# Expert queries of a hybrid decoder step: weights stationary, turned queries straight from the projection

## The chip, the cores and the metric

The kernel runs on one core of a Trainium2 chip. The metric is the device time of one launch in microseconds, the median of several runs; less is better. Matrix products run on TensorE (PE, its weight loads PEld), element-wise work on VectorE (DVE) and ScalarE (ACT), the gathers of expert rows are issued by GpSimd (POOL), and most plain loads by SyncE (SP). All transfers share the core's 16 DMA engines.

## The reference

One layer of a decoder: a token mixer (short convolution and dilated window attention), then a product-key expert layer, for 1024 prompt tokens and 64 sample tokens of width 1024. What the change touches is the expert layer:

```python
def block(xb):                                   # 128 tokens
    q = (xb @ w_query).reshape(PEER_BLOCK, PEER_HEADS, 2, half)      # 8 heads, 2 halves of 128
    s1 = jnp.einsum('thd,kd->thk', q[:, :, 0], sub_keys[0])
    s2 = jnp.einsum('thd,kd->thk', q[:, :, 1], sub_keys[1])
    v1, i1 = lax.top_k(s1, PEER_TOPK)
    v2, i2 = lax.top_k(s2, PEER_TOPK)
    ...                                          # best 16 of the 256 sums -> eidx, gate
    act = jnp.einsum('td,thkd->thk', xb, expert_u[eidx])
    coef = gate * jax.nn.gelu(act)
    return jnp.einsum('thk,thkd->td', coef, expert_v[eidx])
```

Every token reads 8 x 16 rows of `expert_u` and as many of `expert_v`, 4 KB each.

## The kernel before, in words

After a front part (conditioning, first norm, attention inputs), the function `peer` runs everything else as two programs that share the engines.

The **foreground** is 72 jobs, one for each of 9 token tiles (tile 2 holds the 64 sample tokens twice, and its 8 jobs have 8 rows for each partition instead of 16) and 8 heads. Job s ranks scores into expert indices (DVE, `experts`), gathers a u row and a v row for every rank (POOL, lines 1501 and 1511, rings of 8 slots each, u and v alternating in one queue), takes dot products with the u rows (DVE, line 2443), and adds the v rows of job s-1 with their coefficients. About half of the v rows are added by DVE (line 2459), the others by PE as products with a diagonal matrix that ACT makes (line 2107 makes it, line 1787 is the product, 4 records for a row). A v slot comes free when its row is added; a POOL gather that waits for one holds back the gathers behind it.

The **background** makes what the jobs need, in three segments of three tiles: norm, input projections and attention (segments 1 and 2; segment 0's are made in the front part), convolution, `mix`, output projection `out` (line 1729), second norm, `turn` (line 1714, which turns a normed tile into `hT`), and the queries. Its pieces are numbered by `chain_order`, which sets the order on PE, ACT and DVE alike and gives each piece one of six PSUM banks in turn. `Pace` lets each engine go as far into that order as `limit(s, f)` allows at fraction f of job s: `chain_cost` gives each piece a cost, and marks tie job numbers to pieces (everything up to score 6 comes ahead of job 0, the first score of segment g by job 24g - 3, all by job 51). An engine that reaches a piece waits in place, with the rest of its program behind it.

The second norm of a tile is a chain over engines: `add_x` (DVE) after the tile's three `out` chains, `root` (ACT; it also waits until the tile before is stored), `shift_tile` (DVE, last instruction line 2354), then `turn` (PE) and `keep_turned` (ACT). SP stores each tile (`store_tile`) after its shift.

Queries: an item is one head of one tile, and `it` counts them, head by head and within a head tile by tile. In step i, `queries` projects item i with the tile as the stationary operand (line 1756, 8 products of 256 columns, 16 records), ACT copies the result to `qn` (line 2036), PE turns the item before (line 1765, two transposes), ACT copies it to `qT` (line 2044), PE scores the item before that against the sub-keys (line 1773), and ACT copies the scores to one of two `sc_out` buffers (line 2052) and stores them. The third tile's `turn` stands behind the second projection. `load_scores` (line 2063) reads them back for a job. The query weights come in eight blocks of 1 MB, one for each head, by SP (line 1401) into a ring of three slots.

## Time and profile before

| | |
|---|---|
| median of 3 runs | 4194.48 us (4192.9 to 4195.76) |
| profiled execution | 4189.91 us, span 4187.2 us |
| mean granted TensorE clock | 0.882 of full speed |
| busy share of the span | PE 78%, DVE 69%, POOL 59%, PEld 42%, ACT 15% |
| moved by DMA | 1405 MB, mean 336 GB/s |

The profile describes one execution. Its page gives busy time by engine, the span in slices, the chain of work that ended last and groups of instructions; the trace behind it can be asked for stretches (windows), for single instructions in order of time (timeline), and for who waited for whom. A PE row's length holds the pipeline's tail, so the distance between starts tells what a chain takes. The DMA share is the mean busy share of 16 engines; in stretches where transfers never stop it reads up to 1.05.

### The profile page before, as it was taken

Reading aid. Unit: us, or ns where it says so; the run is one execution under the profiler, and the core shown is the slowest. Engines: PE = TensorE matmul, PEld = TensorE weight load, DVE = VectorE, ACT = ScalarE, POOL = GpSimd, SP = SyncE. Lnnn points to the kernel's source line nnn. Section 1 sums busy time; section 2 is a strip of 40 time slices with the busy share of each in tenths; the row PEclk is TensorE's granted clock in tenths of the full one; section 3 lists DMA queues with packets and bytes.
Section 4 is the critical chain, followed back from the end, with each engine's and each line's share of the span. In section 5 each row is a group of like instructions: output and inputs, shape, how many; then the busy total and the mean of one; then the engine's idle time right before and its main releaser. Section 6 shows DMA issues by size and latency. Waiting matters only on the chain. (4 is left out here: it accounts for less than half of the span.)

```text
span 4187.2 us, 33973 instructions
## 1 busy us (share of the span) xinstructions
PE 3280.6 (78%) x9782; PEld 1758.2 (42%) x9798; DVE 2895.2 (69%) x6507; ACT 635.6 (15%) x1759; POOL 2488.9 (59%) x2277
## 2 busy tenths in 40 slices
PE   6978898788888987788888888887777666566666
PEld 1445575654444544455444445444444222222222
DVE  2212111678786777988878987787778788778875
ACT  0020001221012212123110133111111111101010
POOL 0001000477764677567787666876777777777775
PEclk9968898899997899889998898998888888988888
DMA  7316344799997999999999989999999999999998
GB/s 257 124 34 174 98 121 150 277 403 403 393 387 255 331 387 396 352 391 376 401 402 390 385 320 335 390 391 387 387 393 391 373 409 409 408 409 397 405 409 323
DMA packets 578893, 1405.09 MB, mean 336 GB/s; under 512 B 44731, under 2 KB 276347, under 8 KB 578683
## 3 DMA queue, kind: packets, MB, share of 16 engines
q0 software_dynamic: 320080, 1165.57, 71.7%
q1 hardware_dynamic: 223070, 196.45, 15.0%
q10 hardware_dynamic: 35560, 40.91, 2.8%
q8 instruction: 81, 1.33, 0.1%
q14 instruction: 102, 0.84, 0.1%
HBM read 1369.31 MB, written 33.44 MB: 335 GB/s over the span
## 5 line engine op out<-in xcount | busy, mean ns | idle before, releaser
L1787 PE MATMUL peer_psA<-peer_vring,peer_diag 128*128 128x512 f32 x2464 | 1394.8, 706 | 626.4 <-DMA peer_vring<-in_expert_v,peer_idx 474.3
L1501 POOL DMA_INDIRECT peer_uring<-in_expert_u,peer_idx x1088 | 1224.4, 1125 | 713.6 <-DVE peer_idx L2416 360.7
L1511 POOL DMA_INDIRECT peer_vring<-in_expert_v,peer_idx x1088 | 1222.4, 1124 | 548.2 <-issue 301.0
L2443 DVE CUSTOM_DVE_ANT_0 peer_uring<-peer_uring,peer_h 128x1024 f32<-128x1024 f32 x768 | 934.6, 1217 | 218.7 <-DMA peer_uring<-in_expert_u,peer_idx 217.0
L1787 PEld LDWEIGHTS peer_psA<-peer_vring,peer_diag 128*128 128x128 f32 x2464 | 509.6, 221 | 1353.2 <-issue 1165.3
L2459 DVE SCALAR_TENSOR_TENSOR peer_acc<-peer_vring,peer_coef,peer_acc 128x1024 f32<-128x1024 f32 x463 | 593.9, 1283 | 86.2 <-DMA peer_vring<-in_expert_v,peer_idx 80.7
L2443 DVE CUSTOM_DVE_ANT_0 peer_uring<-peer_uring,peer_psB 128x1024 f32<-128x1024 f32 x320 | 388.8, 1215 | 142.8 <-DMA peer_uring<-in_expert_u,peer_idx 142.5
L1682 PE MATMUL peer_psB<-keep_hT,peer_w 128*128 128x384 f32 (+1 forms) x864 | 279.2, 483 | 12.2 <-DMA peer_w<-in_w_in 12.2
L1756 PE MATMUL peer_psB<-peer_w,keep_hT 128*128 128x256 f32 x1152 | 273.4, 393 | 18.4 <-DMA peer_w<-in_w_query 17.3
L1700 PE MATMUL peer_psB<-keep_hT,peer_w 128*128 128x384 f32 (+1 forms) x768 | 250.8, 482 | 20.8 <-DMA peer_w<-in_w_attn_o 20.8
L1756 PEld LDWEIGHTS peer_psB<-peer_w,keep_hT 128*128 128x128 f32 x1152 | 228.5, 200 | 76.5 <-issue 28.2
L2149 ACT ACTIVATE peer_g<-peer_g 128x16 f32<-128x16 f32 (+1 forms) x72 | 15.5, 215 | 1459.7 <-DVE peer_g L2473 1459.7
L1682 PEld LDWEIGHTS peer_psB<-keep_hT,peer_w 128*128 128x128 f32 x864 | 170.4, 198 | 125.8 <-issue 23.9
L1700 PEld LDWEIGHTS peer_psB<-keep_hT,peer_w 128*128 128x128 f32 x768 | 150.4, 197 | 121.4 <-DMA peer_w<-in_w_attn_o 25.0
L2107 ACT ACTIVATE peer_diag<-keep_ident,peer_coef 128x128 f32<-128x128 f32 x616 | 187.8, 388 | 59.8 <-DVE peer_coef L2483 59.8
L1579 PE MATMUL peer_psB<-peer_w,keep_hT 128*128 128x384 f32 x576 | 196.4, 496 | 0.0
L1579 PEld LDWEIGHTS peer_psB<-peer_w,keep_hT 128*128 128x128 f32 x576 | 113.0, 197 | 88.1 <-issue 23.4
L1729 PE MATMUL peer_psB<-peer_w,peer_mT 128*128 128x384 f32 (+3 forms) x432 | 130.6, 461 | 3.0 <-DVE peer_mT L2325 3.0
L1637 PE MATMUL peer_psB<-peer_w,peer_arena 128*128 128x64 f32 x576 | 89.2, 314 | 37.7 <-ACT peer_arena L1967 37.7
L1614 PE MATMUL peer_psB<-peer_w,peer_mT 64*128 64x512 f32 (+3 forms) x224 | 104.9, 552 | 3.4 <-issue 1.8
L1637 PEld LDWEIGHTS peer_psB<-peer_w,peer_arena 128*128 128x128 f32 x576 | 86.3, 232 | 49.1 <-issue 44.6
L1729 PEld LDWEIGHTS peer_psB<-peer_w,peer_mT 128*128 128x128 f32 (+1 forms) x432 | 81.7, 190 | 56.1 <-issue 17.2
(245 smaller groups left out, 2943.8 us busy)
## 6 DMA issues: line engine op xcount, KB each, us to landing
peer_w<-in_w_in SPq DMA_DIRECT2D x102, 512.0 KB, 21.8
peer_w<-in_w_query SPq DMA_DIRECT2D x24, 1024.0 KB, 15.7
peer_w<-in_w_in SPq DMA_DIRECT2D x12, 1536.0 KB, 18.4
peer_uring<-in_expert_u,peer_idx POOLq DMA_INDIRECT x1088, 10.7
peer_vring<-in_expert_v,peer_idx POOLq DMA_INDIRECT x1088, 10.6
front_ring<-in_w_ada POOLq DMA_DIRECT2D x7, 2048.0 KB, 8.3
front_ring<-in_w_ada SPq DMA_DIRECT2D x5, 2048.0 KB, 7.8
peer_w<-in_w_conv_o SPq DMA_DIRECT2D x24, 384.0 KB, 23.1
```

What stands on the lines that cost most here:

```text
L1501: pool.indirect_dma_start(out=uring[:, r % U, :], out_offset=None, in_=io["expert_u"], in_offset=bass.IndirectOffsetOnAxis(ap=idx[:, s % 4 ...
L1511: pool.indirect_dma_start(out=vring[:, r % V, :], out_offset=None, in_=io["expert_v"], in_offset=bass.IndirectOffsetOnAxis(ap=idx[:, s % 4 ...
L1579: last = pe.matmul(dst[:, 0:WQKV], hT[:, k, i * P:(i + 1) * P], wv[:, k, :], start=(k == 0), stop=(k == DC - 1))
L1637: last = pe.matmul(bank(key_o)[:, 0:HD], pT[:, t_slot[g, it, b] % 2, (at % 4) * P:(at % 4 + 1) * P], vv[:, kb, col:col + HD], start=(at == ...
L1682: last = pe.matmul(dst[:, 0:m], wv[:, k, part, :], hT[:, k, 0:m], start=(k == 0), stop=(k == DC - 1))
L1700: last = pe.matmul(dst[:, 0:m], wv[:, KC_AT[q] + k, :], src[:, k, 0:m], start=(k == 0), stop=(k == KC[q] - 1))
L1729: last = pe.matmul(dst[0:R, 0:e - a], mT[:, k, i * P:i * P + R], wv[:, k, :], start=(k == 0), stop=(k == DC - 1))
L1756: last = pe.matmul(dst[:, 0:KD], hT[:, k, j * P:(j + 1) * P], wv[:, k, :], start=(k == 0), stop=(k == DC - 1))
L1787: last = pe.matmul(psA[:, c * 512:(c + 1) * 512], diag[:, a % DG, :], vring[:, r % V, c * 512:(c + 1) * 512], start=first, stop=False, ski ...
L2107: act.activation(diag[:, a % DG, :], ident[:], ACT.Copy, scale=coef[:, s % 4, k:k + 1]).then_inc(diag_set, 1)
L2443: dve.tensor_tensor_reduce(uring[:, r % U, :], uring[:, r % U, :], rows, 1.0, 0.0, ALU.mult, ALU.add, act_[:, k:k + 1]).then_inc(u_used, 1)
L2459: dve.scalar_tensor_tensor(out=acc[:], in0=vring[:, r % V, :], scalar=c, in1=acc[:], op0=ALU.mult, op1=ALU.add).then_inc(v_added, 1)
```

## The change

A head's query weights become the stationary operand: one chain makes one half (128 query columns) of one head for all three tiles, 384 columns at once, and the result comes out turned. So 24 projections of 256 columns and 24 pairs of transposes in a segment become 16 chains `("query", g, h, c)` of 384 columns; `qn` and the transposes go, and ACT copies 16 results of 384 columns to `qT`, where it copied 48 of 256. `qT` now holds four heads and lies in `mT`, the input of the output projection. Scores are still taken by item: the first two of head h-1 stand between the two chains of head h, the third behind them. As a chain reads all three tiles, the third tile's `turn` moves ahead of all queries. `sc_out` has four buffers, and `chain_cost` has 5.1 for a query where it had 3.4 for a projection and 0.5 for a turn.

```diff
+SO = 4
...
-        for i in range(n + 2):
-            if i == 2:
-                order += [("turn", g, SEG - 1, c) for c in range(2)]
-            order += [(name, first + i - lag) for lag, name in enumerate(("project", "turn_q", "score"))
-                      if 0 <= i - lag < n]
+        order += [("turn", g, SEG - 1, c) for c in range(2)]
+        for h in range(HEADS + 1):
+            if h < HEADS:
+                order += [("query", g, h, 0)]
+            order += [("score", (g * HEADS + h - 1) * SEG + i) for i in range(2 if h else 0)]
+            if h < HEADS:
+                order += [("query", g, h, 1)]
+            if h:
+                order += [("score", (g * HEADS + h - 1) * SEG + 2)]
...
-    return {"project": 3.4, "qkv": 5.1, "s": 1.2, "o": 1.5, "t": 0.6}.get(name, 0.5)
+    return {"query": 5.1, "qkv": 5.1, "s": 1.2, "o": 1.5, "t": 0.6}.get(name, 0.5)
...
-    return "project", (g * HEADS + j) * SEG + SEG - 1
+    return "query", g, j, 1
...
-        qn, qT, sc_out = n.sb("qn", [P, 2, K2]), n.sb("qT", [P, 2, K2]), n.sb("sc_out", [P, 2, K2])
+        sc_out = n.sb("sc_out", [P, SO, K2])
+        QS = 4
+        qT = flat[:, 0:QS * 2 * M].rearrange("p (s c m) -> p s c m", s=QS, c=2)
...
             def queries(g):
...
-                        for k in range(DC):
-                            last = pe.matmul(dst[:, 0:KD], hT[:, k, j * P:(j + 1) * P], wv[:, k, :],
-                                             start=(k == 0), stop=(k == DC - 1))
...
-                        for c in range(2):
-                            last = pe.transpose(dst[:, c * P:(c + 1) * P], qn[:, it % 2, c * P:(c + 1) * P], ident[:])
...
+                    for i in range(SEG):
+                        wait_emptied(pe, ("turn", g, i, 1))
+                    dst = opened(key)
+                    for k in range(DC):
+                        last = pe.matmul(dst[:, 0:M], wv[:, k, c * P:(c + 1) * P], hT[:, k, :],
+                                         start=(k == 0), stop=(k == DC - 1))
...
+                yield from turn(g, SEG - 1)
+                for h in range(HEADS + 1):
+                    if h < HEADS:
+                        yield from query(h, 0)
+                    if h:
+                        yield from score(h - 1, 0)
+                        yield from score(h - 1, 1)
+                    if h < HEADS:
+                        yield from query(h, 1)
+                    if h:
+                        yield from score(h - 1, 2)
...
             def norm_root(g, i):
-                yield number["score", (g - 1) * SEG * HEADS + 5 + 5 * i]
+                yield number["score", (g - 1) * SEG * HEADS + 5 + 6 * i]
...
             def keep_queries(g):
...
+                    if h >= QS:
+                        wait_filled(act, ("score", (g * HEADS + h - QS) * SEG + SEG - 1))
+                    act.activation(qT[:, h % QS, c, :], bank(key)[:, 0:M], ACT.Copy).then_inc(out_of(key), 1)
...
+                    if it >= SO:
+                        act.wait_ge(sc_stored[it % SO], 16 * (it // SO))
+                    act.activation(sc_out[:, it % SO, :], bank(key)[:, 0:K2], ACT.Copy).then_inc(out_of(key), 1)
...
             def shift_tile(g, i):
...
-                yield number["out", g, i + 1, 0] if i + 1 < SEG else number["project", g * SEG * HEADS]
+                yield number["out", g, i + 1, 0] if i + 1 < SEG else number["turn", g, SEG - 1, 0]
```

Where this moves instructions on PE, at three places. In these rows line numbers are each kernel's own: before, 1714 is `turn`, 1729 `out`, 1739 the convolution's tail, 1756 the projection, 1765 the transposes, 1773 the scores, 1787 the sum of v rows; after, they are 1721, 1736, 1746, 1759, none, 1770 and 1796. `peer_qT` and `peer_mT` are the turned queries.

Segment 0, ahead of the first job, from the second tile's `turn` on. Before:

```order
L1714 MATMUL peer_psB<-keep_ident,peer_arena 128x128 x8
L1756 MATMUL peer_psB<-peer_w,keep_hT 128x256 x16
L1765 MATMUL peer_psB<-keep_ident,peer_qn 128x128 x2
L1714 MATMUL peer_psB<-keep_ident,peer_arena 128x64 x8
L1756 MATMUL peer_psB<-peer_w,keep_hT 128x256 x8
L1765 MATMUL peer_psB<-keep_ident,peer_qn 128x128 x2
L1773 MATMUL peer_psB<-peer_skT,peer_qT 128x128 x2
L1756 MATMUL peer_psB<-peer_w,keep_hT 128x256 x8
L1765 MATMUL peer_psB<-keep_ident,peer_qn 128x128 x2
```

After:

```order
L1721 MATMUL peer_psB<-keep_ident,peer_arena 128x128 x8
L1721 MATMUL peer_psB<-keep_ident,peer_arena 128x64 x8
L1759 MATMUL peer_psB<-keep_hT,peer_w 128x384 x24
L1770 MATMUL peer_psB<-peer_skT,peer_mT 128x128 x4
L1759 MATMUL peer_psB<-keep_hT,peer_w 128x384 x8
L1770 MATMUL peer_psB<-peer_skT,peer_mT 128x128 x2
L1759 MATMUL peer_psB<-keep_hT,peer_w 128x384 x8
```

The third tile's turn (128x64 x8) goes from behind two projections to ahead of all queries; and score 6, the last piece ahead of job 0, stands behind seven chains of 384 columns, where it stood behind nine of 256.

Segment 1, from the second tile's `turn` on. Before:

```order
L1729 MATMUL peer_psB<-peer_w,peer_mT 128x256 x8
L1714 MATMUL peer_psB<-keep_ident,peer_arena 128x128 x8
L1756 MATMUL peer_psB<-peer_w,keep_hT 128x256 x16
L1765 MATMUL peer_psB<-keep_ident,peer_qn 128x128 x2
L1714 MATMUL peer_psB<-keep_ident,peer_arena 128x128 x8
L1787 MATMUL peer_psA<-peer_vring,peer_diag 128x512 x6
```

After:

```order
L1736 MATMUL peer_psB<-peer_w,peer_mT 128x256 x8
L1721 MATMUL peer_psB<-keep_ident,peer_arena 128x128 x4
L1796 MATMUL peer_psA<-peer_vring,peer_diag 128x512 x2
L1721 MATMUL peer_psB<-keep_ident,peer_arena 128x128 x12
L1796 MATMUL peer_psA<-peer_vring,peer_diag 128x512 x6
L1759 MATMUL peer_psB<-keep_hT,peer_w 128x384 x16
L1796 MATMUL peer_psA<-peer_vring,peer_diag 128x512 x6
```

The third tile's turn follows the second's at once (x12 is half of one and all of the other), and three v rows (x6) stand between it and the first queries.

Segment 2, from the second tile's `turn` on. Before:

```order
L1714 MATMUL peer_psB<-keep_ident,peer_arena 128x128 x8
L1739 MATMUL peer_psB<-keep_ident,peer_tail 18x128 x4
L1787 MATMUL peer_psA<-peer_vring,peer_diag 128x512 x2
L1739 MATMUL peer_psB<-keep_ident,peer_tail 18x128 x2
L1787 MATMUL peer_psA<-peer_vring,peer_diag 128x512 x2
L1756 MATMUL peer_psB<-peer_w,keep_hT 128x256 x8
L1787 MATMUL peer_psA<-peer_vring,peer_diag 128x512 x2
L1756 MATMUL peer_psB<-peer_w,keep_hT 128x256 x8
L1765 MATMUL peer_psB<-keep_ident,peer_qn 128x128 x2
L1714 MATMUL peer_psB<-keep_ident,peer_arena 128x128 x8
L1787 MATMUL peer_psA<-peer_vring,peer_diag 128x512 x6
```

After:

```order
L1721 MATMUL peer_psB<-keep_ident,peer_arena 128x128 x8
L1746 MATMUL peer_psB<-keep_ident,peer_tail 18x128 x6
L1721 MATMUL peer_psB<-keep_ident,peer_arena 128x128 x8
L1796 MATMUL peer_psA<-peer_vring,peer_diag 128x512 x4
L1759 MATMUL peer_psB<-keep_hT,peer_w 128x384 x8
L1796 MATMUL peer_psA<-peer_vring,peer_diag 128x512 x4
L1759 MATMUL peer_psB<-keep_hT,peer_w 128x384 x8
L1796 MATMUL peer_psA<-peer_vring,peer_diag 128x512 x6
```

Two v rows (x2 each) and two projections stood between the second and the third turn; now only the tail's transposes do.

## Rows read from the trace of the kernel before

**Rows 1.** The page, part 2: transfer rate in forty equal slices (about 104.7 us each).

```profile
GB/s 257 124 34 174 98 121 150 277 403 403 393 387 255 331 387 396 352 391 376 401 402 390 385 320 335 390 391 387 387 393 391 373 409 409 408 409 397 405 409 323
```

**Rows 2.** Windows (us): busy us (instructions) of PE, PEld, DVE, ACT, POOL, PEclk, DMA share, GB/s.

```profile
1240.00:1420.00 180.00, 157.89 (x545) 85.63 (x549) 130.81 (x314) 47.65 (x143) 91.08 (x84) 0.79 0.78 277
1420.00:1700.00 280.00, 238.21 (x674) 128.04 (x674) 223.37 (x499) 48.56 (x109) 208.29 (x173) 0.95 1.05 392
1774.00:1990.00 216.00, 174.84 (x683) 122.61 (x684) 181.46 (x436) 59.18 (x155) 148.33 (x123) 0.89 1.00 383
2400.00:2600.00 200.00, 173.94 (x699) 100.77 (x709) 161.26 (x375) 61.17 (x181) 122.83 (x112) 0.87 0.88 318
2900.00:2920.00 20.00, 7.80 (x20) 3.84 (x20) 12.23 (x25) 3.91 (x7) 6.66 (x7) 0.72 0.81 311
2954.00:3262.00 308.00, 234.97 (x769) 142.42 (x770) 241.14 (x531) 56.37 (x172) 244.66 (x208) 0.87 1.01 391
```

**Rows 3.** Timeline before the first gather: start us, us, engine, line, operation [idle before <-releaser].

```profile
720.49 1.22 DVE L2354 TENSOR_TENSOR peer_arena<-peer_arena 64x1024 f32<-64x1024 f32 x1
...
721.82 10.08 PE L1756 MATMUL peer_psB<-peer_w,keep_hT 128*128 128x256 f32 x32 [9.62 <-DMA peer_w<-in_w_query]
...
732.05 0.71 PE L1714 MATMUL peer_psB<-keep_ident,peer_arena 64*128 64x64 f32 x8
...
732.54 1.21 ACT L2019 ACTIVATE keep_hT<-peer_psB 128x256 f32<-128x256 f32 x4
...
738.05 3.62 PE L1756 MATMUL peer_psB<-peer_w,keep_hT 128*128 128x256 f32 x16
...
741.72 0.61 PE L1773 MATMUL peer_psB<-peer_skT,peer_qT 128*128 128x128 f32 x4
...
742.17 3.62 PE L1756 MATMUL peer_psB<-peer_w,keep_hT 128*128 128x256 f32 x16
...
762.30 29.32 SPq L1401 DMA_DIRECT2D peer_w<-in_w_query  x2
...
762.32 0.61 PE L1773 MATMUL peer_psB<-peer_skT,peer_qT 128*128 128x128 f32 x4
...
764.24 1.04 ACTq L2063 DMA_DIRECT2D peer_sc<-key_scores  x2
...
770.01 0.49 DVE L2367 MAX8 peer_v<-peer_sc 128x8 f32<-128x128 f32 x2 [5.92 <-DMA peer_sc<-key_scores]
```

**Rows 4.** Timeline, PE: an output projection chain of 384 columns in segment 1.

```profile
1740.76 5.33 PE L1729 MATMUL peer_psB<-peer_w,peer_mT 128*128 128x384 f32 x16
```

**Rows 5.** Window of 5 us at the first query projection (columns as in the windows above).

```profile
720.00:725.00 5.00, 3.18 (x8) 2.56 (x9) 1.68 (x2) 0.00 (x0) 0.00 (x0) 0.50 1.09 349
```

**Rows 6.** Groups by line and form from 700 us: xcount | busy, mean ns | idle before, releaser.

```profile
L2052 ACT ACTIVATE peer_sc_out<-peer_psB 128x256 f32<-128x256 f32 x72 | 27.4, 381 | 23.4 <-DMA key_scores<-peer_sc_out 13.9 <-PE peer_psB L1773 8.8
```

**Rows 7.** Timeline of segment 1, PE and DVE: second tile's turn to first queries.

```profile
1766.89 1.97 PE L1714 MATMUL peer_psB<-keep_ident,peer_arena 128*128 128x128 f32 x8 [4.59 <-DVE peer_arena L2354]
...
1774.64 9.33 PE L1756 MATMUL peer_psB<-peer_w,keep_hT 128*128 128x256 f32 x32 [5.79 <-DMA peer_w<-in_w_query]
...
1784.90 5.32 PE L1787 MATMUL peer_psA<-peer_vring,peer_diag 128*128 128x512 f32 x12
...
1778.91 1.23 DVE L2354 TENSOR_TENSOR peer_arena<-peer_arena 128x1024 f32<-128x1024 f32 x1
```

**Rows 8.** Timeline of segment 2, PE, POOL and DVE, around the three turns.

```profile
2909.08 1.12 PE L1714 MATMUL peer_psB<-keep_ident,peer_arena 128*128 128x128 f32 x4 [10.60 <-DVE peer_arena L2354]
...
2913.28 0.94 POOL L1511 DMA_INDIRECT peer_vring<-in_expert_v,peer_idx  x1 [11.81 <-PE peer_psA L1787]
...
2945.45 1.97 PE L1714 MATMUL peer_psB<-keep_ident,peer_arena 128*128 128x128 f32 x8 [4.59 <-DVE peer_arena L2354]
...
2948.06 2.76 PE L1787 MATMUL peer_psA<-peer_vring,peer_diag 128*128 128x512 f32 x4
...
2956.07 1.22 DVE L2354 TENSOR_TENSOR peer_arena<-peer_arena 128x1024 f32<-128x1024 f32 x1
```

More of the change, by code:

```diff
@@ new lines, in score @@
+                def score(h, i):
+                    key = ("score", (g * HEADS + h) * SEG + i)
+                    yield number[key]
+                    for c in range(2):
+                        wait_emptied(pe, ("query", g, h, c))
+                    dst = opened(key)
+                    for c in range(2):
+                        last = pe.matmul(dst[:, c * KEYS:(c + 1) * KEYS], qT[:, h % QS, c, i * P:(i + 1) * P],
+                                         skT[:, c, :], start=True, stop=True)
+                    last.then_inc(full(key), 1)
@@ L1883, in keep_norm @@
                     if i == 0 and c == 0:
[L1884 removed]
+                        wait_filled(act, ("query", g - 1, HEADS - 1, 1))
                     wait_filled(act, key)
@@ new lines, in keep_queries @@
+                yield from keep_turned(g, SEG - 1)
+                for h in range(HEADS + 1):
+                    if h < HEADS:
+                        yield from keep_query(h, 0)
+                    if h:
+                        yield from keep_score(h - 1, 0)
+                        yield from keep_score(h - 1, 1)
+                    if h < HEADS:
+                        yield from keep_query(h, 1)
+                    if h:
+                        yield from keep_score(h - 1, 2)
+                    if g + 1 < SEGS_N and h in (2, 4, 6):
+                        yield from norm_root(g + 1, h // 2 - 1)
@@ L2188, in norm_shift @@
             def norm_shift(g, i):
-                yield number["score", (g - 1) * SEG * HEADS + 5 + 5 * i]
+                yield number["score", (g - 1) * SEG * HEADS + 5 + 6 * i]
                 q = SEG * (g - 1) + i
```

91 lines of the change are left out of this document (23 added, 68 removed).

## Prediction

> **What bounds the kernel now.** First the slices of the transfer rate [rows 1]: low and uneven for seven slices, then near 390 to 410 GB/s nearly to the end, with dips in slices 13 and 14, 18, and 24 and 25. Then windows over those dips [rows 2]. A stretch where transfers never stop reads a DMA share of 1.05 (1420 to 1700 us) with PE busy 238 of 280 us, so from the first gather on the transfers set the pace, and other engines matter where they let the share fall. I price that as (1.05 - share) x length. Both attention stretches lose most: (1.05 - 0.78) x 180 = 48.6 us and (1.05 - 0.88) x 200 = 34 us. The stretches with the queries of segments 1 and 2 lose (1.05 - 1.00) x 216 = 10.8 us and (1.05 - 1.01) x 308 = 12.3 us; 20 us at a turn in segment 2 lose (1.05 - 0.81) x 20 = 4.8 us. Last the timelines of the two places where the change can move a transfer: ahead of the first gather, where PE is what everyone waits for [rows 3], and at the turns [rows 7, 8].
>
> So 72 items of cheaper queries are worth little where they lie beside saturated transfers. What counts is when the first gather starts, and how long PE stands still at the moved turn.
>
> **The change, part by part.**
>
> *PE work of the queries.* Before, an item takes 742.17 - 738.05 = 4.12 us [rows 3]: a score 742.17 - 741.72 = 0.45 (its row says 0.61, so a row's tail is 0.16), a projection 3.62 - 0.16 = 3.46, the two transposes the remaining 0.21. Afterwards a chain of 384 columns takes 5.33 - 0.16 = 5.17 us [rows 4]. A segment goes from 24 x 4.12 = 98.9 us to 16 x 5.17 + 24 x 0.45 = 93.5 us: 5.4 us saved, nearly all of it the transposes, for the columns are the same 6144 x 8. PE is busy 175 of 216 us and 235 of 308 us in the two query stretches [rows 2], beside transfers short by 10.8 and 12.3 us. A saving of 3% of PE's busy time there can hardly return more than its own length, 10.8 us in two segments, and it comes in chains of 5.17 us where 3.46 us were the longest a v row had to wait behind. I take -2 us; 0 is one bound, -23 (all of the shortfall of both stretches) the other.
>
> *ACT.* 48 evictions at 0.38 us [rows 6] (a copy of the same size) become 16 of 384 columns, at most 0.38 x 1.5 = 0.57 us: 9 us less in a segment, on an engine busy 59 of 216 us. Its work is hidden under PE's next chain. The two more score buffers can save at most the waits for stores, 13.9 us over the whole run [rows 6], spent on ACT while it has little else to do; if they had cost anything it would be v rows whose diagonals came late. Nothing for both.
>
> *The lead.* Nothing is gathered until score 6 is stored and scores are read back. Before, the first two projections start at 721.82, and score 6 ends at 762.32 + 0.61 = 762.93 [rows 3]. After, the third tile's turn comes first. It is ready at 720.49 + 1.22 = 721.71; turn and eviction took from 732.05 to 732.54 + 1.21 = 733.75, 1.7 us, and at half clock some 0.5 us more, so queries start at 723.9. The granted clock at that point is 0.50 [rows 5], the level of 1.2 GHz, after PE stood idle, and the first 32 products took 10.08 - 0.16 where 2 x 3.46 would do: 3.0 us lost. I let the new kernel lose the same. Then seven chains, 36.2 us, and seven scores, 3.15: 723.9 + 3.0 + 36.2 + 3.15 + 0.16 = 766.4, later by 3.5 us. Half a head more is projected than before (7 chains are 3.5 heads, 9 items are 3). Against it stands a transfer: the sixth block of query weights is issued at 762.30, 1.9 us ahead of the score load at 764.24, which takes until 770.01 [rows 3]. Now its slot is free after the sixth chain, near 760.2, while the score load moves to some 767.7, so most of that megabyte (2.6 us at 400 GB/s) is out of the way. I give 1.5 us for it. Lead: +2.0 us; between -1 (the turn itself wakes the clock, so that 3.0 goes) and +6.5 (the slow stretch is paid twice, round the wait for the evictions). Later gathers only queue behind, so this counts in full.
>
> *The moved turn in segment 1.* Before, PE ended the second turn about 1768.9, stood until weights came at 1774.64, did two projections at low clock (9.33 us), turned the third tile and returned to v rows at 1784.90 [rows 7]. The third tile's shift ended at 1778.91 + 1.23 = 1780.14. After, PE waits for that shift instead, so three v rows follow near 1781.2, some 3.7 us sooner, and the queries later, whose weights have then landed. What is late next is score 24, which job 22 reads; its slack is a job. Net 0; between -4 and +5 (the 4.8 us of a lost window).
>
> *The moved turn in segment 2.* Here v rows are what moves. Before, two v rows started with 2948.06 right behind the second turn of 2945.45, while the third shift ended at 2956.07 + 1.22 = 2957.29 [rows 8]. After, PE stands at the third turn until then, with those rows behind it: 9.2 us. The nearest row for such a stand is the first turn, where PE waited 10.60 us and a gather of v rows 11.81 us [rows 8], which is the window that lost 4.8 us. Three loads of query weights in the same moments fill part of the hole. I take +4; between 0 and +9.2.
>
> *Pacing.* Sixteen costs of 5.1 replace 24 of 3.4 + 0.5, so what follows the queries comes up to five of PE's v rows (over half a job) earlier, while attention keeps its density (24 v rows in segment 1 either way, about 31 in segment 2). The 48.6 and 34 us stay; I allow 4 us either way for where in a job they fall.
>
> **The sum:** -2 + 0 + 2.0 + 0 + 4 + 0 = +4 us. The profiled execution took 4189.91 us (span 4187.2, 2.7 us around it), which gives 4193.9; it lies 4.6 us under the median of 4194.48, so the median to expect is **4198.5 us**. About 0.2%, 8.4 us, is what a measurement of this kernel can tell from no change.
>
> **The rivals.**
>
> *B, faster: the query stretches fill up.* If v rows waited for PE there because of the two round trips through ACT in each item, a path with one round trip, scored a chain later, frees them. For it: 23.1 us of shortfall in the two stretches [rows 2]. Against it: PE stands idle 41 of 216 us and 73 of 308 us there, so it is seldom PE's work that is late. Two thirds recovered, the lead as forecast and the turns free give -15.4 + 2 = -13.4: 4181 us.
>
> *C, slower: the uncovered turn starves the gathers.* Both moved turns hold PE about 10 us with nearly all v rows of a job behind them; eight v slots are then full, and POOL, whose one queue alternates u and v, stops both. It decides once the stop outlasts what is in flight, as at the first turn of segment 2. Upper prices in both segments, 5 + 9.2, with the lead at 5: 4194.5 + 19.2 = 4214 us.
>
> *D, the clock.* PE idle at the moved turns starts each query burst at half clock: 3.0 us for each [rows 3, 5], in two segments, all of it passed on: 4198.5 + 6 = 4204.5 us, slower by 0.24%. Against it: the burst of segment 1 was slow before too, 9.33 us for 6.92 [rows 7], so that price is already in. The Trainium skill, in TensorE: Matmul & The Clock Gate, section Loop structure matters more than you think, warns that a long wait between bursts of products lets the array fall to half clock; by that rule alone D would hold. The trace agrees on the fall (0.50 [rows 5]) but shows it before the change as well.
>
> That the change doesn't do what it says is excluded by the order of PE's instructions.
>
> **How the numbers follow.** The forecast's unknowns (lead -3 to +4.5, turns -4 to +5 each, pacing 4 either way) mostly cancel or add a few us: within 0.2% of no change it has 0.52. B has 0.22, for a shortfall is there to fill and the chain of waits for each item does get shorter; C 0.18; D 0.08. So faster by over 0.2%: 0.22; within: 0.52; slower: 0.18 + 0.08 = 0.26. The range reaches to both rivals' times, 4180 to 4214; the likeliest case alone spans 4190 to 4206.
>
> **What would show it.** Right: the score load of the lead issued 2 to 4 us later than 764.24 and the first gather 0 to 5 us later; PE waiting some 10 us at the third turn of segment 2; a head's queries in about 11.7 us; attention stretches with a share near 0.78 and 0.88. Wrong: a first gather earlier than before, a query stretch at a share of 1.05 (B), a gather of v rows waiting over 15 us at a third turn (C), or attention stretches that gain or lose over 10 us, for which the sum has no term.

## The result, and the profile after

The changed kernel takes **4228.59 us** (median of 5 runs, 4222.43 to 4232.15) beside 4194.62 us of the kernel before on the same chip: ratio 1.008 (95% interval 1.0068 to 1.0093), slower by 34 us and outside the range. Over the chips of this study all runs of the kernel before but one (4290 us) lay between 4177.6 and 4209.4 us, and all of e12's but one (6232 us) between 4171.8 and 4192.2, so single runs less than 15 us apart say little; medians and intervals are compared below.

The profiled execution after (4228.59 us, span 4226.8): from the page, PE's busy time and the transfer rate in forty slices, the counterpart of [rows 1].

```profile
PE 3270.6 (77%) x9253; PEld 1675.7 (40%) x9270; DVE 2893.6 (68%) x6507; ACT 612.3 (14%) x1663; POOL 2482.6 (59%) x2277
...
GB/s 254 123 36 175 93 124 154 291 406 403 391 324 288 349 382 390 311 388 376 406 400 389 353 296 308 389 392 391 388 395 359 390 409 409 409 409 408 393 409 336
```

Slices 17 (311 for 352) and 23 to 25 (353, 296, 308 for 385, 320, 335) are where it got worse; slice 12 (324 for 387) is the first attention stretch, which starts earlier now, and slices 13 and 14 (288 and 349 for 255 and 331) give most of that back. Windows of after (same columns as [rows 2]): the two attention stretches, the two stretches with queries.

```profile
1240.00:1420.00 180.00, 150.82 (x580) 87.95 (x586) 135.54 (x318) 50.72 (x149) 92.25 (x85) 0.81 0.78 276
...
1774.00:1990.00 216.00, 168.99 (x514) 93.05 (x512) 173.34 (x423) 53.20 (x121) 146.45 (x120) 0.88 1.00 379
2400.00:2600.00 200.00, 173.90 (x637) 101.87 (x647) 151.40 (x351) 58.70 (x177) 115.78 (x107) 0.82 0.84 302
...
2954.00:3262.00 308.00, 217.81 (x564) 109.42 (x563) 240.30 (x519) 46.47 (x133) 232.24 (x197) 0.84 1.01 382
```

The first attention stretch and the query stretches read the share that they had. The queries start later in after (at 1789 and 2993 us); windows moved along with them, 1788 to 2004 and 2986 to 3294, read the same 1.00 and 1.01. Two other windows did change: the output projection with the turns of segment 1 (1580 to 1800) and all of segment 2's attention (2360 to 2640). Before:

```profile
1580.00:1800.00 220.00, 171.86 (x501) 97.81 (x500) 188.18 (x445) 42.34 (x91) 142.57 (x123) 0.89 0.99 374
...
2360.00:2640.00 280.00, 246.96 (x938) 141.96 (x947) 230.41 (x528) 79.47 (x234) 183.08 (x164) 0.88 0.93 341
```

After:

```profile
1580.00:1800.00 220.00, 169.63 (x461) 91.80 (x460) 175.82 (x407) 42.47 (x89) 136.57 (x118) 0.88 0.93 349
...
2360.00:2640.00 280.00, 244.95 (x886) 142.06 (x898) 218.40 (x501) 79.39 (x233) 160.47 (x146) 0.82 0.86 309
```

At the prediction's price, (1.05 - share) x length, that is 26.4 - 13.2 = 13 us and 53.2 - 33.6 = 20 us (rounded shares): 33 of the 38.7 us between the two profiled executions, in stretches where the change moved nothing but the third turn of segment 1 and the first queries behind it. Counted in bytes instead (how much later after has moved what before had moved by each of these times, from the rates of 20 us windows), it is 15 and 21 us. Below, *loss* is this price summed over windows of 20 us, each short of 1.045: 10.9 to 24.3 us in the first place ("out 1"), 32.6 to 51.2 in the second ("att 2"), 48.9 to 47.5 in the first attention stretch ("att 1").

**What differs there.** PE in segment 1 before (1729 `out`, 1714 `turn`, 1787 v rows):

```profile
1699.47 10.48 PE L1729 MATMUL peer_psB<-peer_w,peer_mT 128*128 128x384 f32 x32
1709.79 5.31 PE L1787 MATMUL peer_psA<-peer_vring,peer_diag 128*128 128x512 f32 x12
1714.94 3.62 PE L1729 MATMUL peer_psB<-peer_w,peer_mT 128*128 128x256 f32 x16
1725.14 3.78 PE L1787 MATMUL peer_psA<-peer_vring,peer_diag 128*128 128x512 f32 x4 [6.58 <-ACT peer_diag L2107]
1731.35 1.97 PE L1714 MATMUL peer_psB<-keep_ident,peer_arena 128*128 128x128 f32 x8 [2.43 <-DVE peer_arena L2354]
```

And after (1736 `out`, 1721 `turn`, 1796 v rows):

```profile
1709.00 3.78 PE L1796 MATMUL peer_psA<-peer_vring,peer_diag 128*128 128x512 f32 x4 [7.65 <-ACT peer_diag L2115]
1712.58 14.29 PE L1736 MATMUL peer_psB<-peer_w,peer_mT 128*128 128x384 f32 x48
1734.21 1.97 PE L1721 MATMUL peer_psB<-keep_ident,peer_arena 128*128 128x128 f32 x8 [7.35 <-DVE peer_arena L2362]
1735.97 5.91 PE L1796 MATMUL peer_psA<-peer_vring,peer_diag 128*128 128x512 f32 x12
```

All three `out` chains of a tile (x48) now come in one clump with the next turn right behind, and PE adds no v row from 1712.6 to 1736.0; before, v rows stood between the second chain and the third and ahead of the turn. ACT moved as well: `root` (2006) came behind a job's gelu (2149) and the diagonals (2107). ACT before, one tile:

```profile
1723.53 0.21 ACT L2149 ACTIVATE peer_g<-peer_g 128x8 f32<-128x8 f32 x1 [18.28 <-DVE peer_g L2473]
...
1724.68 1.28 ACT L2107 ACTIVATE peer_diag<-keep_ident,peer_coef 128x128 f32<-128x128 f32 x4 [0.94 <-DVE peer_coef L2483]
...
1740.27 1.06 ACT L2006 ACTIVATE peer_arena<-peer_arena 128x1024 f32<-128x1024 f32 x1 [14.02 <-DMA h_before_experts<-peer_arena]
```

Now `root` (2015) stands ahead of a job's gelu (2157), which finds its input ready once the root is done. ACT after, two tiles:

```profile
1738.31 1.06 ACT L2015 ACTIVATE peer_arena<-peer_arena 128x1024 f32<-128x1024 f32 x1 [28.20 <-DMA h_before_experts<-peer_arena]
...
1743.35 0.21 ACT L2157 ACTIVATE peer_g<-peer_g 128x8 f32<-128x8 f32 x1
1744.44 1.28 ACT L2115 ACTIVATE peer_diag<-keep_ident,peer_coef 128x128 f32<-128x128 f32 x4 [0.88 <-DVE peer_coef L2491]
...
1775.55 1.06 ACT L2015 ACTIVATE peer_arena<-peer_arena 128x1024 f32<-128x1024 f32 x1 [29.54 <-PE peer_psB L1721]
```

The pace table says why. PE may go on at a job's start and behind each v row, up to fraction 0.9; in these jobs it has four v rows, so the stops are 0, 0.75 and 0.9. ACT stops at 0.4 (behind the diagonals) and 0.9 (ahead of the gelu), DVE at sixteenths. Worked out from costs and marks, in jobs:

```
                       before                 after
out, tile 0   17.39 17.75 17.997     17.03 17.40 17.65
out, tile 1   18.36 18.73 18.97      18.02 18.39 18.64
turn, tile 0  19.01                  18.68
out, tile 2   19.41 19.78 20.02      19.08 19.46 19.71
turn, tile 1  20.06                  19.74
turn, tile 2  20.65                  19.81
```

Before, the third chain of a tile came due beyond 0.9 (that of tile 2 just past the job's end), so it, its `add_x` and its `root` fell to the next job; after, all three chains fall to PE's stop at 0.75 and the root to ACT's at 0.9 of the same job. A third of a job, some three of its eight v rows, moved them over the job's end.

### The profile page after: what moved, and what is told of

It is laid out like the page before. It is cut to its first block, busy times and chain, and to the rows that moved or that the text cites. A ratio compares the mean times of both kernels' runs of the same rounds, so it can differ in the third digit from the quotient of the medians.

```text
span 4226.8 us, 32651 instructions
## 1 busy us (share of the span) xinstructions
PE 3270.6 (77%) x9253; PEld 1675.7 (40%) x9270; DVE 2893.6 (68%) x6507; ACT 612.3 (14%) x1663; POOL 2482.6 (59%) x2277
## 4 chain that ended last, share of the span: by engine, by line
POOL 19%; DMA 11%; PE 11%; issue 7%; DVE 3%; ACT 1%; ACTq 0%; SPq 0%; DVEq 0%; POOLq 0%
DMA peer_vring<-in_expert_v,peer_idx 10%; POOL peer_vring L1518 10%; POOL peer_uring L1508 9%; PE peer_psA L1796 5%; PE peer_psB L1689 1%; PE peer_psB L1621 1%; PE peer_psB L1644 1%; PE peer_psB L1586 1%; DMA peer_uring<-in_expert_u,peer_idx 1%; PE peer_psB L1736 1%; DVE peer_uring L2451 1%; DVE peer_acc L2467 0%; ACT peer_arena L1957 0%; PE peer_psB L1707 0%; PE peer_psB L1657 0%
## 5 line engine op out<-in xcount | busy, mean ns | idle before, releaser
L1759 PE MATMUL peer_psB<-keep_hT,peer_w 128*128 128x384 f32 x768 | 267.6, 504 | 1.1 <-ACT keep_hT L2028 1.1
L1689 PEld LDWEIGHTS peer_psB<-keep_hT,peer_w 128*128 128x128 f32 x864 | 171.2, 198 | 120.9 <-issue 28.2
L1759 PEld LDWEIGHTS peer_psB<-keep_hT,peer_w 128*128 128x128 f32 x768 | 153.1, 201 | 118.7 <-issue 34.0
L1707 PEld LDWEIGHTS peer_psB<-keep_hT,peer_w 128*128 128x128 f32 x768 | 149.4, 195 | 116.8 <-issue 20.1
L1586 PEld LDWEIGHTS peer_psB<-peer_w,keep_hT 128*128 128x128 f32 x576 | 112.2, 195 | 86.7 <-issue 21.2
## 6 DMA issues: line engine op xcount, KB each, us to landing
peer_w<-in_w_in SPq DMA_DIRECT2D x102, 512.0 KB, 22.9
```

Of the source, the lines that this page charges most:

```text
L1586: last = pe.matmul(dst[:, 0:WQKV], hT[:, k, i * P:(i + 1) * P], wv[:, k, :], start=(k == 0), stop=(k == DC - 1))
L1689: last = pe.matmul(dst[:, 0:m], wv[:, k, part, :], hT[:, k, 0:m], start=(k == 0), stop=(k == DC - 1))
L1707: last = pe.matmul(dst[:, 0:m], wv[:, KC_AT[q] + k, :], src[:, k, 0:m], start=(k == 0), stop=(k == KC[q] - 1))
L1759: last = pe.matmul(dst[:, 0:M], wv[:, k, c * P:(c + 1) * P], hT[:, k, :], start=(k == 0), stop=(k == DC - 1))
```

## The experiments

Rival theories: **pacing** (the cost of queries moves `out` and attention to other places in a job), **the turn** (PE stands at the third turn, ahead of the queries), the four score buffers, and the new chains by themselves. Medians, ratios to the kernel before on the same chip, and losses of the profiled execution:

```
                          us      ratio (95%)             att 1  out 1  att 2
before (profile)       4189.91                             48.9   10.9   32.6
after                  4228.59  1.0080 (1.0068-1.0093)     47.5   24.3   51.2
e1_before_pace         4210.96  1.0026 (1.0013-1.0040)     41.3   16.1   45.2
e2_after_pace          4226.18  1.0063 (1.0046-1.0079)     47.5   23.1   44.2
e3_before_turn         4199.36  1.0018 (1.0002-1.0035)     39.9   10.7   41.8
e4_before_so4          4195.51  0.9996 (0.9980-1.0012)     47.3   11.1   34.8
e5_after_places        4201.16  1.0017 (1.0003-1.0031)     46.3   10.9   32.0
e6_before_places       4225.64  1.0084 (1.0061-1.0108)     46.9   24.1   52.0
e7_late_turn           4191.73  0.9997 (0.9983-1.0011)     46.9   12.9   40.2
e8_split               4202.64  1.0015 (1.0002-1.0029)     47.9   12.1   39.2
e9_attend15            4170.13  0.9941 (0.9919-0.9963)     21.3   10.9   21.2
e10_attend20           4156.01  0.9912 (0.9888-0.9936)     15.9   11.3   12.8
e11_before_attend20    4165.62  0.9937 (0.9920-0.9954)     11.5   10.1   13.4
e12_after_attend20     4179.80  0.9969 (0.9949-0.9988)      6.7   22.9   12.6
e13_after_root_behind  4226.27  1.0081 (1.0054-1.0108)     50.3   20.7   49.2
e14_spread_root_behind 4172.03  0.9950 (0.9932-0.9968)      8.3   23.5   13.0
e15_after_clump_split  4224.13  1.0069 (1.0042-1.0096)     48.1   26.7   40.0
e16_spread_clump_split 4184.90  0.9976 (0.9964-0.9988)      8.7   36.5   15.0
e17_after_all_three    4216.99  1.0053 (1.0034-1.0071)     47.1   12.9   49.6
e18_spread_all_three   4171.01  0.9948 (0.9928-0.9967)      7.9   13.9   14.6
```

A loss comes from one execution. e3 has every piece of attention at its old place and still reads 39.9 and 41.8 where before reads 48.9 and 32.6, so in the attention columns a difference of 9 us says nothing by itself; "out 1" is steadier (10.1 to 12.9 in all kernels with the old places of `out`).

### One part at a time (e1 to e4)

```diff
e1, on before:
+    ... "turn_q": 0.0
e2, on after:
-    return {"query": 5.1, ...
+    return {"query": 5.85, ...
e3, on before (PE; chain_order, keep_turned on ACT and shift_tile's number alike):
+                yield from turn(g, SEG - 1)
                 for i in range(count + 2):
-                    if i == 2:
-                        yield from turn(g, SEG - 1)
e4, on before (shortened; its semaphores and the indices into it alike):
-... n.sb("sc_out", [P, 2, K2])
+... n.sb("sc_out", [P, 4, K2])
```

e1: 

> The kernel before with one number changed: a pair of transposes costs the pace table 0 in place of 0.5, so a segment's queries cost 81.6 as after the change, in place of 93.6, and all that the program does is as before. Pacing theory (the lower cost shifts `out` of segment 1 and attention of segment 2 to other places within a job): slower than before by 15 to 35 us, 4210 to 4230, with the 20 us windows of 1580 to 1800 or of 2360 to 2640 losing 10 us or more beyond before. Turn theory (PE and ACT stand at the third turn ahead of the queries) and any theory that the new chains themselves are slow: within 8 us of 4194.6.

e2: 

> The changed kernel with one number changed: a query chain costs the pace table 5.85 in place of 5.1, so 16 of them cost 93.6, as 24 items did before. Pacing theory: back to 4192 to 4208, with the losses of 1580 to 1800 near 11 and of 2360 to 2640 near 33 us as before. Turn theory: the third turn stands as it stood, 4218 to 4232.

e3: 

> The kernel before with the third tile's turn ahead of the first projection, on PE and ACT, and its shift paced by it; projections, transposes, costs and buffers as before. Turn theory: it carries most of the change's 34 us, 4215 to 4230. Pacing theory: 4190 to 4206, with at most the 3 us of the lead and a stop of 5 to 12 us at a third turn.

e4: 

> The kernel before with four score buffers in place of two and nothing else. The prediction's zero, and both theories: within 5 us of 4194.6. If more stores in flight get in the gathers' way (a third theory): slower by over 8 us.

A number in the pace table alone costs 15 us by the medians and 11 by the ratio (e1), the lower edge of what the pacing theory had; the buffers cost nothing; the turn costs 4 us (1 to 15), its stretch loses what it lost before (10.7), although PE stood 8.52 us at segment 1's third turn: it does not carry most of the 34 us. But e2 did not come back; it missed the pacing theory's numbers and fell within the turn theory's. The sum of the costs was restored, not their place: three chains stand ahead of a segment's first score, to which a mark ties job 21, and at 5.85 each they push `out` still further from that mark, to 17.54, 18.52 and 19.57 for the third chains.

### Places restored, and places moved alone (e5 to e8)

```diff
e5, on after:
+    if name == "query":
+        _, g, h, c = key
+        return 3.733 if (h, c) < (1, 1) else 6.556 if g == 0 else 6.338
e6, on before:
+    if name == "project":
+        g, i = divmod(key[1], SEG * HEADS)
+        return 3.06 if g == 0 else 5.1 if i < SEG else 3.157
+    if name == "turn_q":
+        return 0.0
... (norm_root; norm_shift and ACT's call alike)
-                yield number["score", (g - 1) * SEG * HEADS + 5 + 5 * i]
+                yield number["score", (g - 1) * SEG * HEADS + 5 + 6 * i]
e7, on e5 (PE and ACT alike; 4.7 for the second half of that turn, 2.333 for 3.733):
-                    yield number[key]
+                    yield number["turn", g, i, 1 if i == SEG - 1 else c]
e8, on after:
+        return (6.556, 5.1, 5.1)[g] if (h, c) >= (1, 1) else (3.733, 3.733, 5.1)[g]
```

e5: 

> The changed kernel with costs for the query chains (3.733 for the three ahead of a segment's first score, 6.338 for the rest, 6.556 in segment 0) by which the table lets every piece that is no query, `out` and attention with them, come due at the very row of the job clock at which it came before. Pacing theory (places within a job, which the uniform 5.85 of the run before did not restore: `out` of segment 1 came due 3.7 rows earlier there): 4192 to 4208, 1580 to 1800 losing 9 to 14 us and 2360 to 2640 some 30 to 36 us. Theory that the moved turn or the new chains cost by themselves: 4218 to 4232, 1580 to 1800 losing over 20 us.

e6: 

> The kernel before with costs for its projections (5.1 for the three ahead of a segment's first score, 3.157 for the rest, 3.06 in segment 0, 0 for transposes) by which every piece that is no query comes due at the row of the job clock at which it comes in the changed kernel, and with the norm roots of the next segment spaced as there. Pacing theory: most of the change's loss without the change, 4212 to 4230, with the three `out` chains of a tile in one clump in segment 1. Theory of the turn or the chains: 4190 to 4203.

e7: 

> The kernel of the run e5_after_places with the third tile's turn (PE and ACT) due 3.6 rows of the job clock later, its shift on DVE where it was, so that v rows stand between `out` and that turn. If the moved turn costs what is left over before: 3 to 8 us less than e5_after_places, and PE's stops at the third turns under 4 us in place of 8 to 12. If such stops are covered: the same within 3 us.

e8: 

> The changed kernel with e5_after_places's costs for the queries of segment 0 and for the three chains ahead of segment 1's first score, and 5.1 for all others: pieces of segment 1 come due where they came before, pieces of segment 2 where they come in the changed kernel. If the two places (`out` of segment 1, attention of segment 2) lose apart from each other: half way, 4208 to 4220, 1580 to 1800 losing 9 to 14 us and 2360 to 2640 losing 45 to 55 us. If one stretch's loss only follows from the other's: at 4195 to 4205, or at 4222 and over.

e5 and e6 settle the main question, from both sides. The changed kernel with the old places (e5) is at 4201.2 us, with the old losses (10.9, 32.0); the old kernel with the new places (e6) is at 4225.6, with the new ones (24.1, 52.0), and its PE shows the clump without any of the change:

```profile
1706.27 3.78 PE L1792 MATMUL peer_psA<-peer_vring,peer_diag 128*128 128x512 f32 x4 [7.33 <-ACT peer_diag L2112]
1709.85 14.77 PE L1734 MATMUL peer_psB<-peer_w,peer_mT 128*128 128x384 f32 x48
1731.51 1.97 PE L1719 MATMUL peer_psB<-keep_ident,peer_arena 128*128 128x128 f32 x8 [6.89 <-DVE peer_arena L2359]
```

e7 is 9 us under e5, with intervals that overlap; the stops it was to shorten were 8.53 us in segment 1 (8.51 in e5: the later row falls to the same stop at 0.75) and 3.65 for 5.28 in segment 2, so why it is faster is not shown. e8 missed most of its numbers: segment 1 came back as expected (12.1), but attention of segment 2, at exactly the changed kernel's places, lost 39.2 and not 45 to 55, and 4202.6 us lies in the range of the other theory, that one stretch's loss only follows from the other's. By time e8 is level with e5 (ratios 1.0015 and 1.0017), as if segment 2's new places cost nothing there; e17 below, with those places and segment 1's loss taken back by hand, is at 4217.0 with 49.6, which speaks against that theory. Over the kernels with unspread attention, the old places of segment 2 lost 32.0 to 41.8 (before, e3, e4, e5, e7) and the new ones 39.2 to 52.0 (after, e6, e8, e13, e15, e17; e2 and e1, with other places yet, lost 44.2 and 45.2). So the place is worth some 11 us there by the means (36.3 and 46.9), and another 10 us depend on something that these runs do not separate.

### Attention spread (e9 to e12)

If a piece's cost sets where it falls, it also sets how densely attention is packed. These keep `out`, turns and queries where they are and only stretch attention at the expense of what lies ahead of it and behind it in its segment.

```diff
e10 on e7, e11 on before, e12 on after (e9 on e7: 1.5 with 0.8756 and 0.83):
 def chain_cost(key):
+    cost = piece_cost(key)
+    if len(key) > 2 and key[0] in ("s", "o", "t", "oturn"):
+        return cost * 2.0
+    if len(key) > 2 and key[1] and key[0] in ("qkv", "conv", "mix", "nturn", "rturn"):
+        return cost * {1: 0.7511, 2: 0.66}[key[1]]
+    return cost
```

e9: 

> The kernel of e7_late_turn with the pieces of attention at 1.5 times their cost and those of its segment's input projections, convolution and mixing at 0.876 (segment 1) and 0.83 (segment 2) of theirs: attention is spread over 1.5 times as many jobs, `out`, turns and queries stay due where they were. If attention's loss comes from its density (three to four items a job): 10 to 30 us less than e7_late_turn, 4162 to 4182. If each item costs its stall wherever it falls: 4186 to 4200. If the squeezed projections now hold the v rows up: 4200 and over.

e10: 

> The same with attention at twice its cost and the others at 0.751 and 0.66. If density is what costs: 20 to 45 us less than e7_late_turn, 4147 to 4172, unless the projections, now 1.33 and 1.5 times as dense, stall v rows themselves; that would show as losses between 860 and 1240, 1420 and 1580 or 2000 and 2360, where there were none, and a time above e9_attend15.

e11: 

> The kernel before, with nothing of the change, and the spread of e10_attend20 (attention at twice its cost, input projections, convolution and mixing at 0.751 and 0.66 of theirs). If the gain is the spread's alone: 4150 to 4166, as e10_attend20. If the weight-stationary queries are needed for it, or help once attention no longer loses: 8 us or more above e10_attend20.

e12: 

> The changed kernel as it is (5.1 for every query chain, the third turn right behind `out`) with the same spread. If places within a job matter mainly where background work is dense: attention's part of the loss goes, `out` of segment 1, still in clumps, keeps its 12 us or so: 4164 to 4180, with 1580 to 1800 losing 20 to 26 us. If the spread makes the places not matter at all: 4150 to 4162. If places in attention cost as much as before: 4185 and over.

Density is what costs: 4170 us at 1.5, **4156 us** at 2, faster than both kernels of this case. Windows of e10:

```profile
1240.00:1420.00 180.00, 139.14 (x462) 75.14 (x461) 154.50 (x355) 38.10 (x117) 137.47 (x114) 0.81 0.96 355
1580.00:1800.00 220.00, 177.53 (x496) 96.71 (x495) 187.91 (x458) 44.83 (x97) 140.54 (x119) 0.88 0.99 373
2360.00:2640.00 280.00, 207.39 (x707) 115.25 (x706) 241.58 (x544) 64.59 (x191) 221.28 (x187) 0.80 1.00 374
```

Shares of 0.78 and 0.93 became 0.96 and 1.00. But spread attention reaches beyond these windows, and some of its loss moves there: from 860 to 1580 us e10 loses 21.8 us in all where e7 lost 46.8, and from 2200 to 2900 it loses 29.1 for 40.3. That is 36 us together, as much as the time (4191.7 to 4156.0); most of it is segment 1's. e11 reaches 4165.6 us without the change; its interval overlaps that of e10, so some 10 us of e10's gain may need the new queries, and that is not told apart. e12, with the changed kernel's own places, kept its 22.9 us in segment 1 and came to the top of its range. Its losses fell by more than its time: from 860 to 1240 us, where the projections are now packed closer, it moved 385 GB/s at a share of 1.02 and before 397 at 1.04.

### What in the place costs (e13 to e18)

```diff
     third = {17 + i: number["out", 1, i, 2] for i in range(SEG)}
     def held(s, n):
         return min(n, third[s] - 1) if s in third else n
e13, e14 (ACT, third is called root_at there; the third turn's number for job 19 on PE and DVE):
-                pace.up_to(limit(s, 0.9))
+                pace.up_to(held(s, limit(s, 0.9)))
e15, e16 (PE alone):
-                    pace.up_to(limit(s, min(0.9, (i + 3) / len(rows))))
+                    pace.up_to(held(s, limit(s, min(0.9, (i + 3) / len(rows)))))
e17, e18: held() on PE, ACT and DVE; PE's start of job 20 ends ahead of the third turn
```

e13: 

> The changed kernel with ACT's three norm roots of segment 1 held back from the stop at 0.9 of jobs 17, 18 and 19 to the first stop of the next job, behind its diagonals (the third tile's shift and turn go to job 20 with it); PE still makes the three `out` chains of each tile in one clump. If the root ahead of the gelu is what costs: 1580 to 1800 lose 9 to 15 us in place of 24, and the time is 4208 to 4220. If the clumps on PE cost: the stretch still loses 20 us or more, 4222 to 4232.

e14: 

> The same edit on e12_after_attend20 (the changed kernel with attention spread twice as wide). If the root costs: 1580 to 1800 lose 9 to 15 in place of 23 us, and 4162 to 4172 us. If the clumps cost: 20 us or more, 4174 to 4186.

e15: 

> The changed kernel with PE alone edited: in jobs 17, 18 and 19 the third `out` chain of the tile, and what stands behind it, wait until the next job's start, so that the job's remaining v rows come between the second chain and the third; ACT and DVE keep their places. If PE's absence from v rows is what costs: 1580 to 1800 lose 9 to 16 us in place of 24, and the time is 4210 to 4221. If it is something else (the third turn behind `out`, DVE's or ACT's places): 20 us or more, 4222 to 4232.

e16: 

> The same edit on e12_after_attend20. If PE's absence costs: 9 to 16 in place of 23 us, and 4162 to 4173 us. If something else: 20 us or more, 4172 to 4184.

e17: 

> The changed kernel with the last `out` chain of each tile of segment 1 and all that hangs on it held back to the next job on PE, DVE and ACT alike (PE's third turn behind the first v row of job 20); no cost is changed. If what cost was that the job's end no longer lay between the second chain and the norm: 1580 to 1800 lose 9 to 14 us in place of 24, 4212 to 4220 us. If moving pieces by hand can't restore it (the cost lies in the exact row, or in what came before): 20 us or more, 4222 to 4232.

e18: 

> The same edit on e12_after_attend20. By the first theory: 9 to 14 in place of 23 us, 4163 to 4173 us. By the second: 20 us or more, 4174 to 4188.

Neither single edit gives the loss back. With the root out of the gelu's way (e13), the place still lost 20.7 us: PE leaves v rows for 27 us, and gathers of v rows wait for PE, up to 14.1 us. PE of e13, and the waits of v gathers for PE from 1580 to 1800 (total, times, longest) of before, after and e13:

```profile
1742.44 13.94 PE L1741 MATMUL peer_psB<-peer_w,peer_mT 128*128 128x384 f32 x48
1768.62 1.11 PE L1726 MATMUL peer_psB<-keep_ident,peer_arena 128*128 128x128 f32 x4 [12.25 <-DVE peer_arena L2367]
```

```profile
POOL peer_vring L1511 <- PE peer_psA L1787: 12.9, 7, 7.4
POOL peer_vring L1518 <- PE peer_psA L1796: 48.6, 8, 13.6
POOL peer_vring L1523 <- PE peer_psA L1801: 32.3, 4, 14.1
```

With the clump split on PE alone (e15, 26.7 us; e16 lost even 36.5) no such wait leads POOL's list. But the root still stands ahead of the gelu and now waits 36.5 us there, until the tile before it is stored; gelu and diagonals come behind it, PE's next v row waits 13.75 us for them, and the list is led by u gathers that wait for indices from DVE:

```profile
1745.88 1.06 ACT L2020 ACTIVATE peer_arena<-peer_arena 128x1024 f32<-128x1024 f32 x1 [36.51 <-DMA h_before_experts<-peer_arena]
```

```profile
POOL peer_uring L1513 <- DVE peer_idx L2429: 34.2, 3, 21.5
```

Only all three engines together (e17, e18; pairs were not tried) give the place back: 12.9 for 24.3 us and 13.9 for 22.9, 4217.0 and 4171.0 us, both inside what was expected. The times alone do not part e17 from e13 and e15 (ratios 1.0053, 1.0081 and 1.0069, with intervals that overlap), nor e18 from e14 (4172.0, between the two theories' numbers); the stretch alone (12.9 for 20.7 and 26.7; 13.9 for 23.5) decides. PE of e17 at the second tile has v rows between again:

```profile
1742.43 10.50 PE L1741 MATMUL peer_psB<-peer_w,peer_mT 128*128 128x384 f32 x32
1752.77 5.31 PE L1801 MATMUL peer_psA<-peer_vring,peer_diag 128*128 128x512 f32 x12
1757.92 3.62 PE L1741 MATMUL peer_psB<-peer_w,peer_mT 128*128 128x256 f32 x16
```

POOL's list of e17 is not shorter than that of e15, though; it too is led by u gathers that wait for indices. What differs is what moved meanwhile: in e15's longest stop little (158 GB/s), in e17's three blocks of query weights, which SP issued from 1767.90 on (370 GB/s). The list of e17, then POOL's longest stop in e15 and in e17 as windows (last three: granted clock, DMA share, GB/s):

```profile
POOL peer_uring L1513 <- DVE peer_idx L2429: 36.8, 4, 21.2
```

```profile
1740.00:1761.00 21.00, 8.55 (x16) 4.34 (x17) 9.71 (x21) 6.76 (x14) 0.00 (x0) 0.56 0.39 158
...
1769.00:1790.00 21.00, 10.40 (x21) 5.30 (x20) 10.50 (x16) 4.89 (x8) 0.09 (x1) 0.58 1.03 370
```

So in segment 1 it is shown that the place on all three engines is what costs: the job's end lay between a tile's second chain and its norm, and the cheaper queries moved it away. By which of the waits it costs is read from the traces, not shown by a run.

For segment 2's attention the waits show the same kind of thing, without an experiment that moves one engine. 2360 to 2640 before, then after (total, times, longest):

```profile
ACT peer_arena L1948 <- DVE peer_nm L2242: 79.4, 10, 12.0
POOL peer_vring L1511 <- PE peer_psA L1787: 51.5, 16, 14.0
```

```profile
ACT peer_arena L1957 <- DVE peer_nm L2250: 116.9, 12, 23.8
POOL peer_vring L1518 <- PE peer_psA L1796: 76.4, 15, 13.0
```

ACT's exponentials wait longer for DVE's maxima, and v gathers longer for PE. That this is the way from the place to the loss is argued, not shown.

## Why the prediction was wrong

**Pacing is the step that failed.** The move was seen ("what follows the queries comes up to five of PE's v rows (over half a job) earlier") and sized at 0 with "4 us either way", for density was taken to be all that counts. Measured: 13 us at `out` of segment 1 and 19 us in attention of segment 2, 32 of the 38.7 us between the profiled executions (the lead has 4 more), with 2 us of gains elsewhere from 760 to 3860 us. By e5 and e6 the moved places carry 28 to 31 of the 34 us. The 13 us are explained down to the job's end; of the 19 us the place alone is worth some 11 by the means, e8 has a run in which it cost no time, and the rest stays open. The sentence "attention stretches that gain or lose over 10 us, for which the sum has no term" named the sign that came. What was missing was to hold the table against the stops: third chains at 17.997 and 18.97 stand a few thousandths and hundredths short of a job's end, beyond the last stop, and that could be worked out beforehand.

**The rest of the sum held, in part by balance.** e5, the change without the moved places, is at +6.3 us (ratio 1.0003 to 1.0031) where the sum said +4; but the lead cost 2 us more than forecast, and the 4 us for the turn of segment 2 are not to be seen.

*Lead:* forecast +2.0, measured +4.2. Rows of after that answer to [rows 3]:

```profile
722.81 1.22 DVE L2362 TENSOR_TENSOR peer_arena<-peer_arena 64x1024 f32<-64x1024 f32 x1
...
726.27 17.68 PE L1759 MATMUL peer_psB<-keep_hT,peer_w 128*128 128x384 f32 x48 [1.08 <-ACT keep_hT L2028]
...
749.84 0.61 PE L1770 MATMUL peer_psB<-peer_skT,peer_mT 128*128 128x128 f32 x4
...
761.50 0.61 PE L1770 MATMUL peer_psB<-peer_skT,peer_mT 128*128 128x128 f32 x4
...
769.02 0.95 ACTq L2071 DMA_DIRECT2D peer_sc<-key_scores  x2
...
774.20 0.49 DVE L2375 MAX8 peer_v<-peer_sc 128x8 f32<-128x128 f32 x2 [6.80 <-DMA peer_sc<-key_scores]
```

The third tile's shift (2362, before 2354) came 2.3 us later than before, which nothing in the sum foresaw; the slow first chains cost 17.52 - 15.51 = 2.0 us (3.0 forecast); the load of scores took 5.18 for 5.77 us, 0.6 of the 1.5 us hoped for. It was issued 4.8 us later than before, past the 2 to 4 us named as a sign.

*PE's work:* a head takes 761.50 - 749.84 = 11.66 us, 11.7 as forecast. The query stretches read 1.00 and 1.01 as before, also in the windows that follow them, so rival B falls and the -2 us is not to be seen. *Buffers:* 0, as e4 shows.

*Moved turns:* segment 1's cost nothing in its stretch (e3: 10.7 us lost, 10.9 before). At segment 2's third turn PE stood 12.0 us and a gather 16.3:

```profile
2986.95 1.97 PE L1721 MATMUL peer_psB<-keep_ident,peer_arena 128*128 128x128 f32 x8 [12.03 <-DVE peer_arena L2362]
```

```profile
2991.44 1.17 POOL L1518 DMA_INDIRECT peer_vring<-in_expert_v,peer_idx  x1 [16.30 <-PE peer_psA L1796]
```

That is over the 15 us named as rival C's sign, but the loss from 2900 to 3100 was 7.2 us after and 9.2 before: the sign came and the price did not. The prediction let the loads of query weights fill part of the hole; they filled all of it. Three blocks were issued from 2972.48 on, and the transfers ran on while POOL stood:

```profile
2972.48 10.55 SPq L1408 DMA_DIRECT2D peer_w<-in_w_query  x3
```

```profile
2974.00:2991.00 17.00, 4.97 (x18) 3.10 (x15) 8.24 (x20) 6.02 (x12) 0.94 (x1) 0.53 1.06 382
```

Here the +4 was too much.

*Rival D:* the first two query chains of segment 1 ran from 1789.07 to 1799.39 us, 10.3 us for 2 x 5.17, and those of segment 2 took 5.16 us each, with a granted clock of 1.00 (2.4 GHz) in both places, so no burst behind a moved turn paid the 3.0 us there. In e5 the burst of segment 1 was slow (13.5 us for two chains, granted clock 0.77), and that kernel stands at 4201.2. The mean granted clock fell from 0.882 to 0.875, but to 0.877 in e6, which has no moved turn and no new chains, and it was 0.880 in e2's execution of 4227.7 us: it does not explain the loss.

*A reading:* the dip that the prediction puts in slice 18 stands in slice 17 (352; slice 18 reads 391). Nothing in its sum rests on that.

## What to carry to other kernels

Where a table of costs sets the order of background work, a changed cost is a change of order everywhere behind it: work out where each piece comes due before and after, and hold it against the few points where each engine may go on. A piece that crosses such a point or a job's end moves on several engines at once, and undoing it on one engine only moved the wait here (e13, e15). And where dense background work starves the transfers, its price in that table is a lever of its own: spreading attention twice as wide took 28 us off the kernel before (e11), not much less than the 34 us that the change had cost.

## What the runs showed of the hardware that was not expected

A transfer share near its top is not yet a rate: from 2954 to 3262 us the same share of 1.01 moved 391 GB/s before and 382 after. e12 lost 30.6 us less than before from 760 to 3860 us by its share, but its profiled execution was only 10.3 us shorter.

And how long a gather is held back does not tell its price; what else is being moved does. POOL stood 16.3 us at segment 2's third turn in after while the share was 1.06, and 21.2 us in e17 while it was 1.03, with query weights loading both times; in e15 it stood 21.5 us at a share of 0.39, and in after the clumps of segment 1, with waits of 13 to 14 us, took the share from 1720 to 1740 us down to 0.60.
